# Gate loads of sixteen expert tiles instead of eight in a PEER down stage

## The reference

```python
def peer(xn, wq, subkeys, u, v):
    q = (xt @ wq).reshape(t, PEER_HEADS, 2, D_KEY // 2)
    s = jnp.einsum('thpc,pnc->thpn', q, subkeys)
    # top 16 of 128 keys on each side, top 16 of their sums: 16 of 16384 experts for each of 8 heads
    eidx = ia * N_KEYS + ib
    gate = jax.nn.softmax(cv, axis=-1)
    ...
        hc = jax.nn.gelu(jnp.einsum('chkd,cd->chk', u[ec], xc), approximate=False)
        return jnp.einsum('chk,chkd->cd', hc * gc, v[ec])
```

## Time and profile before

| | us |
|---|---|
| median of 3 runs | 3251.42 |
| lowest and highest | 3246.67, 3253.02 |
| time of the profiled execution | 3249.49 |
| its span | 3247.7 |
| TensorE busy | 3076.2 (95%) |
| VectorE busy | 2541.7 (78%) |
| GpSimd busy | 1822.5 (56%) |
| ScalarE busy | 1383.5 (43%) |

### The profile page before, as it was taken

How to read it: one execution, slowest core, us unless ns; L and a number is a source line. 1 busy time by engine, 2 the same in 40 slices (tenths; PEclk the granted TensorE clock), 3 DMA queues, 4 the chain that set the end, 5 groups by cost and what they waited for, 6 DMA issues and landing times.

```text
span 3247.7 us, 46734 instructions
## 1 busy us (share of the span) xinstructions
PE 3076.2 (95%) x17222; PEld 2785.8 (86%) x17222; DVE 2541.7 (78%) x4953; ACT 1383.5 (43%) x2559; POOL 1822.5 (56%) x1160
## 2 busy tenths in 40 slices
PE   7879999899999999999888899998999999999997
PEld 7879999899998887778775789998999988877776
DVE  7755999977765999999567358989777739989987
ACT  2522343467763333333244233343776643333332
POOL 4543488777773355655130223887777744556652
PEclk9999999899999999999888899999999999999998
DMA  3213499799998999999130122898999989999993
GB/s 109 72 52 96 149 334 337 277 395 391 397 378 318 401 400 399 401 397 379 53 97 1 33 66 79 309 341 298 362 384 398 398 311 396 398 402 399 399 401 136
DMA packets 286579, 920.92 MB, mean 284 GB/s; under 512 B 27344, under 2 KB 77392, under 8 KB 282688
## 3 DMA queue, kind: packets, MB, share of 16 engines
q1 hardware_dynamic: 154336, 415.63, 35.5%
q0 software_dynamic: 111280, 404.77, 32.9%
q10 hardware_dynamic: 20736, 97.53, 7.4%
HBM read 817.34 MB, written 102.38 MB: 283 GB/s over the span
## 4 chain that ended last, share of the span: by engine, by line
PE 68%; DVE 21%; DMA 6%; POOL 2%; issue 1%; ACT 1%; SPq 1%; DVEq 0%; ACTq 0%
PE ps L1682 29%; PE ps L1630 18%; PE ps L1556 10%; PE ps L1662 5%; DMA sring<-s_dram 4%; DVE rowsB L1122 2%; DVE rowsA L1122 1%; DVE cand L1211 1%; DVE cand L1218 1%; DVE slot L1224 1%; DVE xn L941 1%; DVE xl L934 1%; POOL low L597 1%; DMA rowsB<-u,pick 1%; PE ps L1804 1%
## 5 line engine op out<-in xcount | busy, mean ns | idle before, releaser
L755 ACT ACTIVATE high<-raw 128x1024 fp32r<-128x1024 f32 x512 | 542.5, 1059 | 963.6 <-PE ps L1682 638.0
L597 POOL TENSOR_TENSOR low<-raw,high 128x1024 fp32r<-128x1024 f32 x256 | 613.5, 2397 | 227.6 <-ACT high L755 221.3
L1630 PE MATMUL ps<-xh,high 128*128 128x384 f32 x2048 | 700.8, 342 | 10.1 <-POOL low L597 9.9
L1630 PE MATMUL ps<-xh,low 128*128 128x384 f32 x2048 | 688.2, 336 | 0.0
L1630 PE MATMUL ps<-xl,high 128*128 128x384 f32 x2048 | 687.1, 335 | 0.0
L1682 PE MATMUL ps<-high,hh 128*128 128x512 f32 x1536 | 486.6, 397 | 23.7 <-DVE low L1294 23.7
L1682 PE MATMUL ps<-low,hh 128*128 128x512 f32 x1536 | 482.5, 395 | 0.0
L1682 PE MATMUL ps<-high,hl 128*128 128x512 f32 x1536 | 481.1, 394 | 0.0
L588 POOL DMA_INDIRECT rowsB<-v,pick x192 | 289.6, 1508 | 274.5 <-DVE ps L1129 238.0
L588 POOL DMA_INDIRECT rowsA<-v,pick x192 | 300.3, 1564 | 221.2 <-DVE ps L1129 215.2
L1630 PEld LDWEIGHTS ps<-xh,high 128*128 128x128 f32 x2048 | 387.1, 189 | 14.3 <-POOL low L597 13.4
(11 more groups left out here) (279 smaller groups left out, 5146.7 us busy)
## 6 DMA issues: line engine op xcount, KB each, us to landing
raw<-uT SPq DMA_DIRECT2D x256, 512.0 KB
raw<-v SPq DMA_DIRECT2D x256, 512.0 KB
gate_dram<-gblk ACTq DMA_DIRECT2D x24, 2048.0 KB
gt<-gate_dram SPq DMA_DIRECT2D x32, 1536.0 KB
s_dram<-sring ACTq DMA_DIRECT2D x120, 384.0 KB
sring<-s_dram SPq DMA_DIRECT2D x120, 384.0 KB
raw<-wts SPq DMA_DIRECT2D x74, 512.0 KB, 3.6
rowsB<-u,pick POOLq DMA_INDIRECT x192
```

Source lines behind the costliest of these rows:

```text
L597: pool.tensor_tensor(low[:, m % 4], raw[:, m % 4], high[:, (m + 2) % 3].bitcast(F32), ALU.subtract).then_inc(sem("lo_ready"), 1)
L755: act.activation(high[:, (m + 2) % 3], tile_raw(m), ACT.Copy).then_inc(sem("hi_ready"), 1)
L1630: ins = pe.matmul(ps[:, m % 2, 0:DN], w[:, c], x[:, c, 0:DN], start=(c == 0 and k == 0), stop=(c == NC - 1 and k == 2))
```

## The change

A gate tile now holds sixteen expert tiles (`GE = 16`). Gate tiles 0, 2, 4 and 6 go to `gt`, which is one buffer of the same 24 KB. Gate tiles 1, 3, 5 and 7 go to two buffers: blocks 0 to 7 to `gtA`, in the place of `xh` and `xl` beside the output's copies, and blocks 8 to 11 to `gtB`, behind the ring of `v`. Gate tile 0 is loaded in two halves of eight expert tiles, at the places in SyncE's order where gate tiles 0 and 1 were loaded before; gate tile 1 is loaded behind the eighth `v` tile, when the up stage is done. Later gate tile g + 2 is issued in step j = 16g + 12. A gate tile in two buffers is multiplied by two instructions of VectorE, the second of which is held until the first is done. `hh`, `hl` and `raw2` move to the end of `gt`.

```diff
-GE = 8
+GE = 16
+NGA = 8
...
-        gt = Span(nc, top_at, gblk_at).take("gt", [P, 2, NGB, GE * GB])
+        st = Span(nc, top_at, gblk_at)
+        gt = st.take("gt", [P, NGB, GE * GB])
+        down_at = st.at
...
-        st = Span(nc, gblk_at, SB_HI)
+        st = Span(nc, down_at, SB_HI)
         hh = st.take("hh", [P, 3, DN], F32R)
         hl = st.take("hl", [P, 3, DN], F32R)
...
+        gtB = st.take("gtB", [P, NGB - NGA, GE * GB])
...
         accS1 = st.take("accS1", [P, D])
+        gtA = st.take("gtA", [P, NGA, GE * GB])
...
                 def load_gates(g):
-                    spq.dma_start(gt[:, g % 2], gate_dram[l].rearrange("b p (g n) -> p b g n", n=GE * GB)
-                                  [:, :, turned_tile(g * GE) // GE]
-                                  ).then_inc(sem(f"gt_loaded{g % 2}"), 16)
+                    cols = slice(turned_tile(g * GE) * GB, (turned_tile(g * GE) + GE) * GB)
+                    blocks = gate_dram[l].rearrange("b p n -> p b n")[:, :, cols]
+                    if g % 2 == 0:
+                        spq.dma_start(gt[:, :, :], blocks).then_inc(sem("gt_loaded0"), 16)
+                    else:
+                        spq.dma_start(gtA[:, :, :], blocks[:, 0:NGA]).then_inc(sem("gt_loaded1"), 16)
+                        spq.dma_start(gtB[:, :, :], blocks[:, NGA:]).then_inc(sem("gt_loaded1"), 16)
+
+                def load_first_gates(h):
+                    n = turned_tile(h * KEPT)
+                    spq.dma_start(gt[:, :, h * KEPT * GB:(h + 1) * KEPT * GB],
+                                  gate_dram[l].rearrange("b p n -> p b n")[:, :, n * GB:(n + KEPT) * GB]
+                                  ).then_inc(sem(("gt_first", "gt_loaded0")[h]), 16)
...
-                load_gates(0)
+                load_first_gates(0)
                 for n in range(4):
                     load_v(n)
                 for q in range(4):
                     spq.wait_ge(sem("mm_done"), after("mm_done", l, KEYS - 3 + q))
                     load_v(q + 4)
                     if q == 0:
-                        load_gates(1)
+                        load_first_gates(1)
+                load_gates(1)
...
-                    dve.wait_ge(sem(f"gt_loaded{n // GE % 2}"), after("gt_loaded", l, 16 * (n // GE // 2 + 1)))
                     hb = sring[:, n // 2 % 4, n % 2].rearrange("p (b t) -> p b t", b=NGB)
-                    dve.tensor_tensor(hb, hb, gt[:, n // GE % 2, :, n % GE * GB:(n % GE + 1) * GB], ALU.mult
-                                      ).then_inc(sem("h_mul"), 1)
+                    cols = slice(n % GE * GB, (n % GE + 1) * GB)
+                    if n // GE % 2 == 0:
+                        if n < KEPT:
+                            dve.wait_ge(sem("gt_first"), after("gt_first", l, 16))
+                        else:
+                            dve.wait_ge(sem("gt_loaded0"), after("gt_loaded", l, 16 * (n // GE // 2 + 1)))
+                        dve.tensor_tensor(hb, hb, gt[:, :, cols], ALU.mult).then_inc(sem("h_mul"), 1)
+                    else:
+                        dve.wait_ge(sem("gt_loaded1"), 2 * after("gt_loaded", l, 16 * (n // GE // 2 + 1)))
+                        chain.did(dve.tensor_tensor(hb[:, 0:NGA], hb[:, 0:NGA], gtA[:, :, cols], ALU.mult))
+                        chain.settle()
+                        dve.tensor_tensor(hb[:, NGA:], hb[:, NGA:], gtB[:, :, cols], ALU.mult
+                                          ).then_inc(sem("h_mul"), 1)
```

More of the change, by code:

```diff
@@ L186 @@
     "sc_read": 2 * PH, "scS_read": PH // 2, "ss_done": PH // 2, "ex_in": 3 + ND, "ex_out": 2 + ND, "turned": ND, "slot_ready": ND, "slots": ND,
-    "hot": DN // 4, "ones_made": DN // 4, "iota_ready": 1, "g_done": DN // 4, "g_copied": DN // 4, "g_stored": 16 * NGB // 2, "gt_loaded": 16 * KEYS // GE // 2,
+    "hot": DN // 4, "ones_made": DN // 4, "iota_ready": 1, "g_done": DN // 4, "g_copied": DN // 4, "g_stored": 16 * NGB // 2, "gt_loaded": 16 * KEYS // GE // 2, "gt_first": 16,
     "phid_ready": 2, "y_copied": 3, "a_copied": 1, "y_turned": NC, "y_added": NC + 1,
```

## The result

The changed kernel takes 3280.22 us (median of 6 runs, 3277.43 to 3291.61); the kernel before took 3252.46 beside it (6 runs, 3246.67 to 3255.26). The ratio is 1.0094, 95% interval 1.0079 to 1.0110: slower by 28 us, where 9 were forecast, and outside the forecast's range of 3244 to 3272. (The ratio and its interval are estimated from the single runs, so a ratio can differ a little from the quotient of two medians.)

A forecast was written before the change was run, and what follows sets the result against it. Down stages were taken as TensorE's chain, broken by late hidden pairs while gate loads fill the DMA. 3249.5 + 8.8 (4.4 a layer, split multiply free) = 3258.3, median 1.9 higher, so 3260 us; range 3244 to 3272.

The forecast's parts named there:

- The bound and the mechanism: Down stages: gate loads in SyncE's queue make hidden pairs late, VectorE waits, then TensorE; q1 has 56% of the engines.
- Packet prices: Gate loads: 49 ns for a 1 KB packet, 87 for 2 KB; DMA lighter by 7 us in 545 a layer.
- VectorE: Split gate multiply: 0.41 and 0.28 us, 0.18 more for each of 64 tiles a layer, hidden, so no cost.
- Two waits, at tiles 7 and 21: Down stage: 8.4 us lost plus 3.8 for the clock, 12.2 in place of 7.8, +4.4 a layer.
- The queue does not run dry, so extra work in front is not absorbed: SyncE's queue: 7.4 us more in front of the pair of tiles 22 and 23 makes it land 13.2 us later.
- Once lost this time is slack for every later pair: Down stage after the first waits: TensorE's lost 8.4 us counts as slack for all later hidden pairs.
- the late waits of before should vanish: Down stage near j = 84: 59.8 us of loads against 61.1 before, so pairs land earlier and late waits go.
- the start: Down stage's first 56 tiles: 2.5 us lost at the clock's lower level of 1.2 GHz, which stay.
- The clock's price: Down stage: after each of two long waits the clock stands at 0.50, costing 1.9 us each, 3.8 a layer.
- Longer packets win: Rival, gate loads: 1 KB packets cost 67 ns, 2 KB 98, so faster, 3246 or 3236 us; chance 0.18.
- no change: Rival, SyncE's queue: VectorE's waiting gives q1 75.8% of the engines, -0.9 us a layer, 3250; chance 0.25.
- VectorE becomes the bound: Rival, split multiply: 0.42 us more a tile, 6.4 a layer on top, 3273 us; chance 0.07.

The follow-up runs named there:

- e8: Changed kernel with gate tiles in e2's spaced pieces, each as two loads of eight tiles in 1 KB packets; 3254.97 us, ratio 1.0012 to the kernel before.
- e2: Changed kernel with each 3 MB gate tile in six 512 KB loads at spaced steps, same 2 KB packets; 3245.63 us, ratio 0.9966 to the kernel before.
- e1: Kernel before with only VectorE's gate multiply split in two instructions on every second stretch of sixteen tiles; 3257.21 us, ratio 1.0005.
- e6: Changed kernel with only gate tile 1 spread over steps 0 to 5, later gate tiles still 3 MB loads; 3288.14 us, ratio 1.0103 to before.
- e13: Changed kernel with its 3 MB gate loads issued by ScalarE on a queue of their own; 3248.65 us, ratio 0.9989 to the kernel before.
- e9: Changed kernel with each gate tile in two 1.5 MB loads eight steps apart, 2 KB packets; 3246.79 us, ratio 0.9985 to the kernel before.

## Why the prediction was wrong

- **The bound and the mechanism: right.** Hidden pairs behind a gate load in SyncE's queue, through VectorE to TensorE. q1's share behind the burst was 55.5%, forecast 56%.
- **Packet prices: right.** 2 KB packets took 87 ns in the trace of after (mean of the 10752 of a down stage), as forecast. e8 against e2 gives 5.3 us a stage where the prices give 7. What it buys is less than what the burst costs.
- **VectorE: right.** Its busy time is 2564.5 us in place of 2541.7, 22.8 / 128 = 0.18 us for each split tile as forecast; 418 and 292 ns against 0.41 and 0.28. e1 confirms that it hides.
- **Two waits, at tiles 7 and 21: right place, too large.** Forecast 8.4 + 3.8 = 12.2 us a layer; measured 4.7 to 4.9 and 1.7 to 2.6 in four stages, 7.0 on the mean. The sum took for tile 22 that all loads since the stage began still stood in the queue ("The queue does not run dry, so extra work in front is not absorbed"). By 1062 to 1082 the queue of after was as good as empty, since the wait at tile 7 had let it drain (e6, without that wait, has the backlog and loses 7.7 there). So what was late at tile 21 was this one burst and not 7.4 us more of a backlog.
- **The step that failed:** "Once lost this time is slack for every later pair ... and the late waits of before should vanish." It counts loads over the whole stage, as if TensorE's delay were stored. But SyncE holds `v` and hidden loads to TensorE's pace, so after a wait the next loads go out later too. What a wait leaves is an emptier queue, which serves the next load at most (e6); with or without it the queue has run nearly empty before the loads behind that one (the last `v` load ahead of that of 1219.63 landed after 6.4 us, in e6 ahead of its next gate load after 5.7), and each can make the pairs behind it late anew. Measured: of 559.3 - 535.0 = 24.3 us lost a stage, 2.1 at the start, 7.0 in the first two waits, and 15.2 later, where the forecast had 0. Against the forecast's 14.7 (2.5 + 12.2) these are -0.4, -5.2 and +15.2, 9.6 us more. Before loses 10.4 (10.3 in the forecast), so the stage grew by 13.9 us in place of 4.4.
- **That it came out slower at all is luck.** Start and two waits as measured, 9.1 us, are less than the 10.4 that before loses: with no later waits the stage would have been 1 us shorter. The sign was right only because the two waits were forecast too large; what made the kernel slower are the later waits, which were forecast as nothing.
- **Held issues: missing.** The sum has no term for SyncE itself. After a gate load its next issues were held 3.4 us past the pair's due time here (7.6 us for two `v` issues that take 4.5 elsewhere). Of the 23.4 us of the first pair that is a seventh, but more than the 2.6 us lost. Two things speak against it as a cause of its own. While these issues were held (1086.5 to 1094.2 us) q1 kept moving packets at 53.0% of the engines, so a pair issued sooner would still have stood behind the same bytes; and the kernel before has the longer holds (up to 10.8 us against 6.4) and the smaller loss. No run takes away the hold alone: e13 takes away both.
- **The clock's price: right in size, but it does not follow every wait.** Windows of after (columns as in the earlier trace rows), behind the waits that ended at 1055.44, 1259.33 and 1392.87:

```profile
1056.00:1058.00 2.00, 2.00 (x6) 1.54 (x5) 2.00 (x3) 0.52 (x1) 1.01 (x1) 0.50 1.03 409
...
1260.00:1262.00 2.00, 2.00 (x11) 1.59 (x10) 2.00 (x3) 0.72 (x2) 0.60 (x1) 1.00 1.03 409
```

```profile
1394.00:1396.00 2.00, 2.00 (x6) 1.60 (x5) 1.97 (x5) 0.52 (x1) 0.95 (x1) 0.50 1.01 402
```

 The lower level of 1.2 GHz stood behind tiles 6 and 84, which lost 1.7 us more each at the next tile, not behind tile 52 (0.5). TensorE had stood still for 3.1, 2.3 and 2.5 us, so the length of the wait alone does not decide it. Of the two prices that were forecast, 1.9 at tile 7 and 1.9 at tile 21, the first came (1.7), the second did not (0.5).
- **Rivals.** "Longer packets win" and "no change" fell because they looked at bytes and at one pair; q1's share, which both put at 76%, was 55.5% behind the burst. "VectorE becomes the bound", the only slower rival, came near in size (3273) with the wrong mechanism.

## What to carry to other kernels

In a queue that serves in order, cost a large load by what stands behind it: take the worst pair after each load, from its due time to its landing, and not the load's average share. If nobody waits for the large load soon, cut it into pieces at spaced steps, or give it a queue of its own; here 512 KB pieces turned a change of +28 us into one of -8 (medians; the ratio makes it -11). Time that a consumer loses is slack for the next load at most, when the loads are held to that consumer's pace.

## What the hardware showed

- An issue on SyncE can be held for a long time behind a load of many packets: up to 10.8 us in layer 0's stage of before and 6.4 in after (1536 packets of 1 and 2 KB); behind e9's loads of 768 packets the longest was 4.2 us. The size of the load is not all of it: with e2's loads of 256 packets it was 4.6.
- Three queues on full engines moved 1296, 1279 and 1315 packets in 30 us and got 39.6, 37.5 and 24.1% of the engines, the smallest share with the shortest packets; moving 3 MB from one to another cut the `v` loads' time to land by 40% with no byte less.
- In e6 the waits behind later loads were larger than in after's first profile and like those of its second (564.4 / 560.9 against 561.9 / 563.7). What makes the same kernel's stages differ by 7 us stays open.
